# One wait a block for TensorE's weight halves, in place of one for the bank and one for each half

## The chip, the cores and the metric

The kernel runs on one core of a Trainium2 chip. The metric is the device time of one execution in microseconds; lower is better. The runs' times are of unprofiled executions; the profile is of one execution more.

## What is computed

One layer of a hybrid decoder for 256 prompt tokens and 8 sample tokens, 264 rows of 2048 features in all, in float32:

```
x = x + 1/2 * SwiGLU_1(rmsnorm(x))                    # 2048 -> 2 x 5632 -> 2048
h = rmsnorm(x);  P = h @ w_in                         # RWKV-7 columns | attention q,k,v | branch gates
A = RWKV-7 time mixing;  B = dilated window attention
x = x + (sigmoid(gA) * (A @ w_branch_rwkv) + sigmoid(gB) * (B @ w_branch_attn)) @ w_out
x = x + 1/2 * SwiGLU_2(rmsnorm(x))
```

Nearly all of TensorE's time goes into the products with the weights. To keep float32 precision with the float32r format of TensorE, each weight and each activation is split into a high part (rounded to float32r) and a low part (the rest), and each product of two 128-row tiles is three matmuls: high x high, high x low and low x high.

## The kernel before, in words

**Blocks, halves, quarters.** The weights are cut into 397 blocks, one for each 128 output features of a phase. A block has KT tiles of 128 x 128 (16 in most phases, 12 in the last part of each FFN's second matrix, 8 in `ba`, 6 in `bb`). It accumulates in one of four PSUM banks (`result`, block number modulo 4). The phases are, in order: `ffn1_in0`, `ffn1_out0`, `ffn1_in1`, `ffn1_out1`, `ffn1_in2`, `ffn1_out2`, `lora`, `qkv`, `rkv`, `gates`, `bb`, `ba`, `out`, and the six of the second FFN. A block is loaded in two halves. Half h of block b is unit u = 2b + h. A half of 16-tile blocks is 8 tiles, so 24 matmuls of 264 columns. `products` can also do a block's quarters apart, so that other work of TensorE stands between them; `rkv` and `gates` use this.

**The stream of a unit.** There are four slots (`RING`) for a unit's raw weights, high part and low part: `raw`, `whi`, `wlo`. SyncE's queue loads unit u into `raw` once the low part of unit u-4 has been made (`lo_done`). ScalarE's `split_hi` copies it to `whi`, once it has landed and TensorE is done with unit u-4 (`half_done`). VectorE's `split_lo` subtracts to make `wlo` and raises `lo_done`. TensorE multiplies and raises `half_done` at the end of each half.

**Order on ScalarE and VectorE.** The order is written out by hand. At step n of a phase each of the two first calls `ahead`, which splits the two units 2b + 3 and 2b + 4 (b is the block of step n, `LOOK` is 3), and then does what block n leaves: VectorE evicts the bank and raises `evac`. So the low part of unit 2b + 1 is made in the step of block b - 1, after the eviction of block b - 2 in most phases and of block b - 4 in all. In the first phase of each FFN the normalisation comes in between: TensorE sums the squares (`sums_pe`, line 335) after block 2, ScalarE takes the root and VectorE the reciprocal, and only then VectorE evicts blocks 0, 1 and 2 (`hidden` with n == 2), with ScalarE's `gate_silu` for blocks 0 and 2 in the same step. In step 0 of the first FFN ScalarE squares the second half of x and VectorE adds up the squares (`x_squares_dve`, lines 309 to 313).

**In the middle of the layer.** `qkv` has four groups of four small matmuls of TensorE (line 1268) that wait for ScalarE's sigmoids of the last group. In `rkv` TensorE does attention between the halves of some blocks: scores (line 1444), transposes (line 1456), values. When `bb` is done, GpSimd's queue loads the residual x back from memory (line 645), which VectorE needs in `out`.

**Loops.** `walk` runs most blocks of a phase in a hardware loop of four blocks a turn, so the thresholds of the waits hold a register there. Blocks outside the loops wait for constants.

Of the kernel before, what the change touches and what calls it, by code (L numbers as in the profile page):

```python
# [63 lines left out]
BODY = 4  # L64
# [98 lines left out]
def build(nc, ins, outs, side, xs):  # L163
    with ExitStack() as ctx:
# [11 lines left out]
        def sem(name):  # L176
            return ctx.enter_context(nc.semaphore(name))
# [29 lines left out]
        lo_done = sem("lo_done")  # L207
        half_done = sem("half_done")
        evac = sem("evac")
# [7 lines left out]
        act, dve, pe = nc.scalar, nc.vector, nc.tensor  # L217
# [23 lines left out]
        def products(name, n, i, parts, before=None, quarters=(0, 1, 2, 3)):  # L241

            b = FIRST[name] + n
            tiles = [(bank, k, kt, xhi, xlo) for bank, kt, xhi, xlo in parts for k in range(kt)]
            assert len(tiles) == KT_OF[b]
            h = len(tiles) // 2
            if 0 in quarters:
                pe.wait_ge(evac, b + 1 + BODY * i)
            for q in quarters:
                u = 2 * b + q // 2  # L250
                if q % 2 == 0:
                    pe.wait_ge(lo_done, u + 1 + 2 * BODY * i)
                for c in range(h // 2, h) if q % 2 else range(h // 2):
                    bank, k, kt, xhi, xlo = tiles[q // 2 * h + c]
                    if before is not None:
                        before(q // 2 * h + c)
                    hi, lo = (t[:, u % RING, c * P:(c + 1) * P] for t in (whi, wlo))
                    pe.matmul(bank[:, 0:T], hi, xhi[:, k], start=(k == 0), stop=False)  # L258
                    pe.matmul(bank[:, 0:T], hi, xlo[:, k], start=False, stop=False)  # L259
                    mm = pe.matmul(bank[:, 0:T], lo, xhi[:, k], start=False, stop=(k == kt - 1))  # L260
                if q % 2:
                    mm.then_inc(half_done, 1)
# [83 lines left out]
        def ffn_pe(f, r):  # L346
            for q, kt in enumerate(FFN_PARTS):
                first = q == 0
                pairs = (FT if f == 2 else 0) + sum(FFN_PARTS[:q])

                def hidden_there(k):
                    if k == 0 or k >= kt - 2:
                        pe.wait_ge(mid_done, pairs + max(k + 1, kt - 2))

                def up_down(n, i):
                    products(f"ffn{f}_in{q}", n, i, [(result(f"ffn{f}_in{q}", n), DT, hhi, hlo)],
                             h_there(r) if n == 0 and first else None)
                    if n == 2 and first:
                        sums_pe(r)
                walk(pe, f"ffn{f}_in{q}", up_down, BODY if first else 0)  # L360
                walk(pe, f"ffn{f}_out{q}", lambda n, i: products(
                    f"ffn{f}_out{q}", n, i, [(result(f"ffn{f}_out{q}", n), kt, mhi, mlo)],
                    hidden_there if n == 0 else None))
# [853 lines left out]
        def stream(name, hi, lo, before=None):  # L1217
            walk(pe, name, lambda n, i: products(name, n, i, [(result(name, n), KT_OF[FIRST[name]], hi, lo)],
                                                 before if n == 0 else None))
# [525 lines left out]
```

## Time and profile before

| | |
|---|---|
| median of 3 runs | 2451.45 us (2451.36 to 2454.17) |
| profiled execution | 2462.51 us, span 2460.7 us |
| TensorE busy | 2408.8 us, 98% of the span |
| VectorE busy | 1476.6 us, 60% |
| ScalarE busy | 974.7 us, 40% |
| mean granted TensorE clock | 0.985 |
| DMA | 428.27 MB, 174 GB/s |
| the chain that ended last | TensorE 92%, VectorE 3%, ScalarE 2%, DMA 2% |

Times in the trace are microseconds from the start of the span. A row of the timeline begins with an instruction's start and its duration; matmuls overlap in the pipeline, so a matmul of 0.28 us is followed by the next after 0.12 us. In brackets stands how long the engine was idle before, and what ended that.

### The profile page before, as it was taken

How to read it: one execution, taken by the hardware profiler on the slowest of the kernel's cores; microseconds unless marked ns; L12 is line 12 of the kernel's file. 1: busy time of each engine (PE TensorE's matmuls, PEld its weight loads, DVE VectorE, ACT ScalarE, POOL GpSimd, SP SyncE). 2: the span in 40 equal slices, each digit the busy share in tenths (PEclk: the TensorE clock that was granted, in tenths of full speed). 3: DMA queues.
4: the chain of work that ended last, by engine and by line, in shares of the span. 5: the costliest groups of instructions: out<-in, count | busy, mean ns of one | idle time of the engine just before them, and what ended most of it. 6: DMA issues, size and time to landing. Idle time of an engine off the chain costs nothing.

```text
span 2460.7 us, 57958 instructions
## 1 busy us (share of the span) xinstructions
PE 2408.8 (98%) x23350; PEld 2376.8 (97%) x23350; DVE 1476.6 (60%) x2071; ACT 974.7 (40%) x1233; POOL 81.4 (3%) x134
## 2 busy tenths in 40 slices
PE   7999999999999999979999999999999999999999
PEld 7999999999999999968999989999999999999999
DVE  6555555545567496666555585766555455555554
ACT  5333334333345543344222244644433333333333
POOL 0000000000013000000000000021000000000000
PEclk9999999999999999889999999999999999999999
DMA  6666566555556644323422454665555555555555
GB/s 236 207 226 201 183 226 228 182 182 183 179 162 231 210 156 138 106 97 126 144 80 80 147 174 133 217 193 169 192 186 180 180 182 181 183 180 180 183 167 172
DMA packets 122612, 428.27 MB, mean 174 GB/s; under 512 B 14296, under 2 KB 20568, under 8 KB 121440
## 3 DMA queue, kind: packets, MB, share of 16 engines
q1 hardware_dynamic: 117504, 393.49, 48.7%
q0 software_dynamic: 4960, 32.61, 3.9%
q8 instruction: 117, 1.92, 0.3%
q14 instruction: 31, 0.25, 0.0%
HBM read 415.17 MB, written 21.33 MB: 177 GB/s over the span
## 4 chain that ended last, share of the span: by engine, by line
PE 92%; DVE 3%; ACT 2%; DMA 2%; DVEq 1%; issue 1%; SPq 0%; ACTq 0%
PE bank L258 28%; PE bank L259 28%; PE bank L260 28%; PE bank L1225 4%; DVE wlo L231 1%; DMA raw<-in_weights 1%; ACT whi L225 1%; PE bank L1382 0%; PE bank L1420 0%; DMA x<-in_x 0%; PE bank L1549 0%; PE bank L1568 0%; PE bank L1561 0%; DVE nrm L1052 0%; DVE pr L1062 0%
## 5 line engine op out<-in xcount | busy, mean ns | idle before, releaser
L231 DVE TENSOR_TENSOR wlo<-raw,whi 128x1024 fp32r<-128x1024 f32 (+3 forms) x794 | 914.7, 1155 | 666.0 <-ACT whi L225 663.0
L258 PE MATMUL bank<-hhi,whi 128*128 128x264 f32 x4048 | 1171.1, 289 | 12.6 <-DVE hlo L294 12.6
L259 PE MATMUL bank<-hlo,whi 128*128 128x264 f32 x4048 | 1154.2, 285 | 0.0
L225 ACT ACTIVATE whi<-raw 128x1024 fp32r<-128x1024 f32 (+3 forms) x794 | 793.1, 1001 | 908.4 <-PE bank L260 880.2
L260 PE MATMUL bank<-hhi,wlo 128*128 128x264 f32 x4048 | 1152.8, 285 | 0.0
L258 PEld LDWEIGHTS bank<-hhi,whi 128*128 128x128 f32 x4048 | 769.9, 190 | 24.6 <-DMA ones<-in_ones 12.6
L259 PEld LDWEIGHTS bank<-hlo,whi 128*128 128x128 f32 x4048 | 770.5, 190 | 0.9
L260 PEld LDWEIGHTS bank<-hhi,wlo 128*128 128x128 f32 x4048 | 766.3, 189 | 0.0
L258 PE MATMUL bank<-mhi,whi 128*128 128x264 f32 x1408 | 399.5, 284 | 0.0
L260 PE MATMUL bank<-mhi,wlo 128*128 128x264 f32 x1408 | 399.0, 283 | 0.0
L259 PE MATMUL bank<-mlo,whi 128*128 128x264 f32 x1408 | 398.9, 283 | 0.0
L259 PEld LDWEIGHTS bank<-mlo,whi 128*128 128x128 f32 x1408 | 265.3, 188 | 0.0
L258 PEld LDWEIGHTS bank<-mhi,whi 128*128 128x128 f32 x1408 | 265.2, 188 | 0.0
L260 PEld LDWEIGHTS bank<-mhi,wlo 128*128 128x128 f32 x1408 | 264.0, 188 | 0.0
L372 ACT ACTIVATE silu<-gated 128x264 f32<-128x264 f32 x88 | 37.3, 424 | 203.7 <-DVE gated L417 203.7
L433 DVE SCALAR_TENSOR_TENSOR x<-bank,x 128x264 f32 (+1 forms) x96 | 41.5, 433 | 58.8 <-PE bank L260 58.8
L258 PE MATMUL bank<-mghi,whi 128*128 128x264 f32 x256 | 72.6, 284 | 0.0
L259 PE MATMUL bank<-mglo,whi 128*128 128x264 f32 x256 | 72.5, 283 | 0.0
L260 PE MATMUL bank<-mghi,wlo 128*128 128x264 f32 x256 | 72.5, 283 | 0.0
L417 DVE TENSOR_TENSOR gated<-bank,rstd 128x264 f32<-128x264 f32 x88 | 38.1, 433 | 48.0 <-PE bank L260 47.9
L288 ACT ACTIVATE hhi<-x,gains 128x264 fp32r<-128x264 f32 (+1 forms) x48 | 23.4, 512 | 77.0 <-DVE x L1019 40.3
L294 DVE SCALAR_TENSOR_TENSOR hlo<-x,gains,hhi 128x264 fp32r<-128x264 f32 (+1 forms) x48 | 32.4, 695 | 33.0 <-ACT hhi L288 32.9
(279 smaller groups left out, 1789.2 us busy)
## 6 DMA issues: line engine op xcount, KB each, us to landing
raw<-in_weights SPq DMA_DIRECT2D x666, 512.0 KB, 3.3
raw<-in_weights SPq DMA_DIRECT2D x64, 384.0 KB, 3.1
out_skv<-in_cache POOLq DMA_DIRECT2D x16, 512.0 KB, 3.9
raw<-in_weights SPq DMA_DIRECT2D x32, 256.0 KB, 2.8
raw<-in_weights SPq DMA_DIRECT2D x32, 192.0 KB, 2.5
side<-stg POOLq DMA_DIRECT2D x18, 132.0 KB, 3.6
gates<-side POOLq DMA_DIRECT2D x1, 2376.0 KB, 14.7
x<-in_x SPq DMA_DIRECT2D x4, 528.0 KB, 7.2
```

Of the source, the lines that this page charges most:

```text
L225: act.activation(whi[:, u % RING, 0:n], raw[:, u % RING, 0:n], ACT.Copy).then_inc(hi_done, 1)
L231: dve.tensor_tensor(wlo[:, s, 0:n], raw[:, s, 0:n], whi[:, s, 0:n].bitcast(F32), ALU.subtract).then_inc(lo_done, 1)
L258: pe.matmul(bank[:, 0:T], hi, xhi[:, k], start=(k == 0), stop=False)
L259: pe.matmul(bank[:, 0:T], hi, xlo[:, k], start=False, stop=False)
L260: mm = pe.matmul(bank[:, 0:T], lo, xhi[:, k], start=False, stop=(k == kt - 1))
L288: act.activation(hhi[:, m], x[:, m], ACT.Copy, scale=gained(r, n, i)).then_inc(hhi_done, 1)
L294: dve.scalar_tensor_tensor(hlo[:, m], x[:, m], gained(r, n, i), hhi[:, m].bitcast(F32), ALU.mult, ALU.subtract).then_inc(h_done, 1)
L372: act.activation(silu[:, n // 2 % 2], gated[:, n // 2 % 2], ACT.Silu).then_inc(silu_done, 1)
L417: dve.tensor_tensor(gated[:, slot], result(name, n)[:, 0:T], rstd[:], ALU.mult).then_inc(evac, 1)
L433: dve.scalar_tensor_tensor(x[:, m], result(out, n)[:, 0:T], 0.5, x[:, m], ALU.mult, ALU.add).then_inc(evac, 1)
L1225: mm = pe.matmul(out, lhs(j, p ^ frm), rhs(j, p ^ frm), start=(t == 0), stop=(t == len(terms) - 1))
```

## The change

Before, TensorE waits at the start of a block until the bank is free (`evac`), then for the low part of the block's first half, and in the middle for the low part of its second half. The low parts are made in order, so that the count that tells of the second half's tells of the first half's too, and VectorE's order puts the eviction of the bank's last block before it. After the change TensorE waits once, at the start of the block, until the low part of the second half is there. Block 0 is left as it was for its halves: it waits for its first half at its start and for its second in the middle.

```diff
@@ -244,12 +244,14 @@
             h = len(tiles) // 2
+
+
             if 0 in quarters:
-                pe.wait_ge(evac, b + 1 + BODY * i)
+                pe.wait_ge(lo_done, 2 * b + (2 if b else 1) + 2 * BODY * i)
             for q in quarters:
                 u = 2 * b + q // 2
-                if q % 2 == 0:
-                    pe.wait_ge(lo_done, u + 1 + 2 * BODY * i)
+                if q == 2 and b == 0:
+                    pe.wait_ge(lo_done, 2)
                 for c in range(h // 2, h) if q % 2 else range(h // 2):
```

## Rows read from the trace of the kernel before

**Rows 1.** The page: the span, and TensorE's line of busy times.

```profile
span 2460.7 us, 57958 instructions
...
PE 2408.8 (98%) x23350; PEld 2376.8 (97%) x23350; DVE 1476.6 (60%) x2071; ACT 974.7 (40%) x1233; POOL 81.4 (3%) x134
```

**Rows 2.** TensorE's sequencer at the lines of the waits: count, then ns min/median/max.

```profile
L252 PEldq ALU_OP  x441: 32/32/42, 38.7 to 2436.2; - x147
L252 PEldq EVENT_SEMAPHORE  x143: 51/51/51, 10.0 to 2451.4; - x143
...
L248 PEldq ALU_OP  x189: 32/32/32, 41.9 to 2434.0; - x189
```

**Rows 3.** Timeline of TensorE: the last matmuls of three halves in a row.

```profile
310.76 0.28 PE L260 MATMUL bank<-hhi,wlo 128*128 128x264 f32 x1
...
313.66 0.28 PE L260 MATMUL bank<-hhi,wlo 128*128 128x264 f32 x1
...
316.56 0.28 PE L260 MATMUL bank<-hhi,wlo 128*128 128x264 f32 x1
```

**Rows 4.** Timeline, second FFN part: a second half's split, and its block's first matmul.

```profile
301.35 1.23 DVE L231 TENSOR_TENSOR wlo<-raw,whi 128x1024 fp32r<-128x1024 f32 x1 [1.44 <-ACT whi L225]
...
305.08 0.28 PE L258 MATMUL bank<-hhi,whi 128*128 128x264 f32 x1
```

**Rows 5.** Timeline, first stage: block 2's first matmul, its second half's split.

```profile
25.95 0.28 PE L258 MATMUL bank<-hhi,whi 128*128 128x264 f32 x1
...
26.67 1.22 DVE L231 TENSOR_TENSOR wlo<-raw,whi 128x1024 fp32r<-128x1024 f32 x1
```

**Rows 6.** Timeline, first stage, block 4: first matmul, split, its middle's two matmuls.

```profile
38.00 0.28 PE L258 MATMUL bank<-hhi,whi 128*128 128x264 f32 x1
...
39.76 1.23 DVE L231 TENSOR_TENSOR wlo<-raw,whi 128x1024 fp32r<-128x1024 f32 x1 [1.44 <-ACT whi L225]
...
41.04 0.39 PE L258 MATMUL bank<-hhi,whi 128*128 128x264 f32 x1
41.26 0.28 PE L259 MATMUL bank<-hlo,whi 128*128 128x264 f32 x1
```

**Rows 7.** Timeline, second FFN, block 4: first matmul, second half's split.

```profile
1715.32 0.28 PE L258 MATMUL bank<-hhi,whi 128*128 128x264 f32 x1
...
1716.65 1.23 DVE L231 TENSOR_TENSOR wlo<-raw,whi 128x1024 fp32r<-128x1024 f32 x1 [1.44 <-ACT whi L225]
```

**Rows 8.** Timeline, bb, blocks 2 and 14: second half's split, first matmul.

```profile
1513.33 0.55 DVE L231 TENSOR_TENSOR wlo<-raw,whi 128x384 fp32r<-128x384 f32 x1
...
1513.54 0.28 PE L258 MATMUL bank<-obh,whi 128*128 128x264 f32 x1
...
1539.76 0.56 DVE L231 TENSOR_TENSOR wlo<-raw,whi 128x384 fp32r<-128x384 f32 x1
...
1540.02 0.28 PE L258 MATMUL bank<-obh,whi 128*128 128x264 f32 x1
```

**Rows 9.** Timeline of TensorE, ba, block 2: first matmul, first of the second half.

```profile
1550.25 0.29 PE L258 MATMUL bank<-oah,whi 128*128 128x264 f32 x1
...
1556.81 0.59 PE L258 MATMUL bank<-oah,whi 128*128 128x264 f32 x1 [4.94 <-DVE wlo L231]
```

**Rows 10.** Timeline, out, block 0: second half's split, first matmul.

```profile
1598.32 1.22 DVE L231 TENSOR_TENSOR wlo<-raw,whi 128x1024 fp32r<-128x1024 f32 x1
...
1598.84 0.28 PE L258 MATMUL bank<-mghi,whi 128*128 128x264 f32 x1
```

**Rows 11.** Timeline of TensorE: stalls in qkv and in rkv.

```profile
819.68 1.82 PE L1268 MATMUL bank<-lora,w2a 64*128 64x264 f32 x8 [2.08 <-ACT wlog L676]
...
1059.17 1.22 PE L1444 MATMUL bank<-qkv 64*128 64x128 f32 x4 [9.13 <-ACT pt L849]
```

**Rows 12.** Stretches: us, engines' busy us and counts, granted clock, DMA, GB/s.

```profile
821.70:825.20 3.50, 3.50 (x18) 3.50 (x18) 2.71 (x3) 2.41 (x5) 0.00 (x0) 0.51 0.74 209
...
1555.60:1562.40 6.80, 5.59 (x25) 5.59 (x26) 5.37 (x11) 4.09 (x9) 0.00 (x0) 0.50 0.49 156
```

## The prediction

> **What bounds the kernel now.** I read the page first. The span is 2460.7 us and TensorE is busy in 98% of it [rows 1]; the reader is to see that no other engine can be the bound of the whole, so that any time in which TensorE now stands still, or stops standing still, goes into the result almost one for one. The profiled execution took 2462.51 us with what lies around its span, the median of the runs is 2451.45 us; I work out a difference in the profiled execution and add it to the median.
>
> Then the sequencer side of the waits: what the removed instructions cost. In the looped blocks the thresholds are computed in registers, and the trace shows these as operations of TensorE's sequencer: 189 at the line of the bank's wait, 441 at the line of the half's wait, of 32 ns each, and 143 stand-alone waits of 51 ns [rows 2]. Then the pace of the matmuls. The last matmul of a half starts at 310.76, that of the next half at 313.66, of the one after at 316.56: 2.90 us for 24 matmuls both times, 120.8 ns for one [rows 3]. The first of the two halves is the second of its block, which waits once; the other begins a block, and a turn of the loop as well, and waits twice. They take the same time. So the sequencer runs ahead of the matmuls and what it does for a wait that is already met costs nothing.
>
> Then how early the low parts are ready. A wait costs only if the split is late, so I set the end of each of VectorE's 794 operations that write the low part beside the first matmul of the block that it belongs to. The pattern of most blocks is [rows 4]: the low part of the second half of the block that starts at 305.08 ended at 301.35 + 1.23 = 302.58, 2.50 us before the block began. Waiting for it at the start of the block is free there. But in 15 of the 397 blocks the second half's low part ends after the block has started. The kernel of before hides that behind the first half's matmuls. The changed one doesn't.
>
> **The change, part by part.**
>
> The bank's wait goes. VectorE evicts the bank's last block before it makes the low part now waited for, so the new wait implies it, and TensorE never idled for an eviction before one of these blocks. Its sequencer work is worth nothing by [rows 3]. The least it can be worth is nothing; the most, if each register operation and wait delayed the matmuls by its whole duration, is 189 x 32 ns, half of 441 x 32 ns and 143 x 51 ns [rows 2], 20.4 us. I take nothing, since the two equal halves are the same case and the bound is not.
>
> The first half's wait is implied by the second's. The second half's wait moves to the start of the block. What queues behind it are the first half's 24 matmuls (9 to 18 where the blocks are shallower), and for these halves ScalarE's next split of the slot waits, then VectorE's, then SyncE's next load. Nothing moves on SyncE's or GpSimd's queue. Block 0 keeps its two waits.
>
> So the price is a sum over the late blocks. For each: the end of the low part, less the start of the block, plus the 0.05 us in which TensorE takes the news (40.99 to 41.04 in [rows 6]), less the stall in the middle that goes away.
>
> First stage, blocks 1 and 2. Block 2 starts at 25.95; its second low part runs from 26.67 to 27.89, behind VectorE's sums of squares of x [rows 5]: 1.99 us. Those sums hang on x's load and not on TensorE, so the smaller lateness of block 1 is inside this.
>
> First stage, block 4. Starts at 38.00; low part 39.76 to 40.99; the middle stall of before was 41.04 less 38.00 less 2.90, 0.14 us [rows 6]. Price 3.04 - 0.14 = 2.90 us. Why it is late decides whether this adds to the last one: ScalarE's and VectorE's order puts the root, the reciprocal and the first gate blocks ahead of this split, and all of them wait for the sum that TensorE makes after block 2. The chain moves with block 2, so it adds. Block 5 is late by 1 us as well, but its low part doesn't wait for block 4's matmuls, and the 2.90 us cover it.
>
> Second FFN, block 4: the same chain. Start 1715.32, low part 1716.65 to 1717.88 [rows 7]: 2.61 us. Block 5 is covered again.
>
> bb, blocks 2 and 14: 1513.54 against 1513.88, and 1540.02 against 1540.32 [rows 8]: 0.39 and 0.35 us.
>
> ba, block 2. Here GpSimd's queue issues x's reload, the whole residual, once bb is done, and the weights land behind it. TensorE starts the block at 1550.25, does its first half of 12 matmuls, and stands until 1556.81, 4.94 us of it idle [rows 9]. Now it stands from the start of the block until the same 1556.81, and the 12 matmuls, 12 x 0.1208 = 1.45 us, come after. ba's block 0 is late too (0.9 us), but this stall takes that up.
>
> out, block 0: 1598.84 against 1598.32 + 1.22 = 1599.54 [rows 10]: 0.75 us.
>
> lora's block 2 (0.1 us) and qkv's block 2 (0.7 us) stand before a stall of 2.08 us in which TensorE waits for ScalarE, itself held by weights that land late; rkv's blocks 12 and 13 (1.5 us, since TensorE's transposes stand between the halves there) before one of 9.13 us on ScalarE's and VectorE's attention chain [rows 11]. These I cost at nothing: the cover is those stalls, and without it they would be 2.3 us.
>
> A restart: after a stall the second matmul comes 0.22 us behind the first (41.04 to 41.26) in place of 0.12 [rows 6]. Five of the stalls are new (first block 2, second FFN, the two of bb, out): 5 x 0.10 = 0.50 us.
>
> Sum: 1.99 + 2.90 + 2.61 + 0.39 + 0.35 + 1.45 + 0.75 + 0.50 = 10.94 us. 2451.45 + 10.94 = 2462.4 us, and about 2473.5 us for a profiled execution.
>
> **The clock, weighed against a rule.** After this stall of 4.94 us in ba the granted clock is 0.50 (1.2 GHz) for 6.80 us, with 25 matmuls in it [rows 12]; at full clock these take 25 x 0.12 = 3.0 us of the 5.59 us that they took, so the drop costs about 2.6 us. After the stall in qkv and the few small matmuls behind it the clock was 0.51 over 3.50 us [rows 12], with 18 matmuls where 3.50 / 0.12 = 29 would fit: 11 x 0.12 = 1.3 us. The stalls that my forecast adds to the FFN are 3.0 and 2.6 us long, between these two, with dense matmuls on either side. The Trainium skill (TensorE: Matmul & The Clock Gate, HAM oscillation) has waits between bursts of matmuls put the engine back to the lower clock, burst after burst; it speaks against this change. By it each of the two long stalls would also cost a drop; the trace has that after its longest stalls, and none with an isolated stall of 3 us, so it doesn't decide.
>
> **The rivals.**
> A, my forecast: the stalls as summed, no new drop of the clock. 2462.4 us.
> B, the clock falls as well. For it: the two rows of [rows 12]. Against: the new stalls are shorter than ba's, and isolated. 1.3 to 2.6 us for each of the two: 2463.7 to 2467.6 us, with one of them at the mean price 2464.3.
> C, the lateness that hangs on transfers is a thing of the profiled execution, which took 11 us longer than the median. Then the first block 2, bb's block 14, ba and out lose little, and what the order of the engines' own work makes late stays: 2.90 + 2.61 + 0.39 and two restarts, 6.1 us: 2457.6 us. Against: the weights pass the same queues without the profiler.
> D, the other side: faster. TensorE's sequencer is late somewhere, and the matmuls pay for its instructions. From 11 us of such instructions on it outweighs the stalls; at its 20.4 us the time is 2451.45 - 20.4 + 10.9 = 2442.0 us. Against: the two equal halves [rows 3].
> E, the change loses next to nothing: VectorE's chain ahead of block 4 turns out not to move with block 2, or shifts are taken up in later stalls as in [rows 11]. Half of the sum gone, under 4.9 us: about 2455 us.
>
> **How the numbers follow.** A 0.51, B 0.27, C 0.10, D 0.04, E 0.08. The likeliest is A. The range reaches from C's time to B's upper one, 2457.5 to 2467.6, and leaves out D, E and a part of B and C. A measurement of this kernel can tell about 0.2%, 4.9 us, from no change: A, B and C are slower by more, E is within, D is faster. Slower 0.88, same 0.08, faster 0.04.
>
> **What the changed kernel's profile would show.** Right: TensorE's first matmul of block 2 about 0.05 us after the end of the low part, near 27.9, and no idle in the middle of a block past block 0; a stall of 3 us ahead of block 4 in both FFNs; in ba the stall of before moved from the middle of block 2 to its start, with 24 matmuls after it; fewer sequencer operations at the two lines and the same 2.90 us from half to half. Wrong: halves shorter than 2.90 us (D); block 4 starting on time (E); new stretches at 1.2 GHz behind the FFN stalls (B). What would make the number wrong while the mechanism holds is that transfers land at other times, and that a stretch of low clock begins or ends elsewhere than before.

## The result

The changed kernel takes 2468.22 us (median of 6 runs, 2466.71 to 2474.78), the kernel before 2452.55 us (median of 6, 2449.93 to 2462.33): slower, ratio 1.0063, interval 1.0043 to 1.0083, or 10.5 to 20.4 us. The forecast was 2462.4 us, 2457.5 to 2467.6. The sign, the mechanism and the larger stalls were right; the median lies 0.6 us above the range, whose upper end was rival B's. The profiled execution took 2474.78 us, 12.3 us more than the profiled one of before.

The page of the changed kernel, to [rows 1]: 652 instructions fewer, and TensorE busy 5.8 us longer with the same 23350 matmuls.

```profile
span 2473.0 us, 57306 instructions
...
PE 2414.6 (98%) x23350; PEld 2381.1 (96%) x23350; DVE 1477.7 (60%) x2071; ACT 975.8 (39%) x1233; POOL 81.4 (3%) x134
```

The sequencer's operations at the line of the one wait, to [rows 2]. The 441 operations and 143 stand-alone waits at the halves' line are gone.

```profile
L250 PEldq ALU_OP  x189: 32/32/42, 46.3 to 2446.3; - x189
```

Three halves in a row, to [rows 3]. 2.90 us for each, as before, though most of the sequencer's work for the waits is gone: it had cost nothing.

```profile
315.17 0.28 PE L262 MATMUL bank<-hhi,wlo 128*128 128x264 f32 x1
...
318.07 0.28 PE L262 MATMUL bank<-hhi,wlo 128*128 128x264 f32 x1
...
320.97 0.28 PE L262 MATMUL bank<-hhi,wlo 128*128 128x264 f32 x1
```

What TensorE waited for, over the whole execution: us in total, times, the longest.

```profile
PE bank L1446 <- ACT pt L851: 20.0, 3, 7.8
PE bank L260 <- DVE wlo L231: 12.7, 7, 3.7
...
PE bank L1332 <- issue: 0.5, 1, 0.5
PE bank L1227 <- issue: 0.2, 1, 0.2
```

Waits for a low part are now seven, 12.7 us; the kernel before had one, of 4.94 us ([rows 9]). Here are the matmuls behind six of the seven, and the splits that the first two waited for, to [rows 5] to [rows 10].

```profile
26.09 1.22 DVE L231 TENSOR_TENSOR wlo<-raw,whi 128x1024 fp32r<-128x1024 f32 x1
...
27.36 0.39 PE L260 MATMUL bank<-hhi,whi 128*128 128x264 f32 x1 [1.07 <-DVE wlo L231]
...
41.26 1.23 DVE L231 TENSOR_TENSOR wlo<-raw,whi 128x1024 fp32r<-128x1024 f32 x1 [1.44 <-ACT whi L225]
...
42.54 0.39 PE L260 MATMUL bank<-hhi,whi 128*128 128x264 f32 x1 [2.87 <-DVE wlo L231]
...
1521.65 0.40 PE L260 MATMUL bank<-obh,whi 128*128 128x264 f32 x1 [0.24 <-DVE wlo L231]
...
1565.31 0.59 PE L260 MATMUL bank<-oah,whi 128*128 128x264 f32 x1 [3.74 <-DVE wlo L231]
...
1606.76 0.39 PE L260 MATMUL bank<-mghi,whi 128*128 128x264 f32 x1 [0.97 <-DVE wlo L231]
...
1725.93 0.39 PE L260 MATMUL bank<-hhi,whi 128*128 128x264 f32 x1 [2.45 <-DVE wlo L231]
```

Each is the first matmul of a block, and starts 0.05 us after the split ends (41.26 + 1.23 = 42.49, then 42.54). They are block 2 and block 4 of the first FFN, block 2 of bb, block 3 of ba (the forecast had block 2), block 0 of out, block 4 of the second FFN. The seventh is rkv's block 12, and what follows it is to [rows 11]:

```profile
1045.96 0.39 PE L260 MATMUL bank<-hhi,whi 128*128 128x264 f32 x1 [1.37 <-DVE wlo L231]
...
1063.73 0.58 PE L1446 MATMUL bank<-qkv 64*128 64x128 f32 x1 [7.81 <-ACT pt L851]
```

The stall of 9.13 us in block 13 is now 7.81 us: it took up the 1.37 us, as forecast.

The clock, in four stretches of the changed kernel, to [rows 12]: two in gates, one after the other, one in ba behind the stall, and one behind the second FFN's stall.

```profile
1227.00:1232.30 5.30, 5.30 (x102) 5.08 (x99) 1.97 (x4) 1.54 (x2) 0.54 (x1) 1.00 0.44 153
1232.40:1235.80 3.40, 3.40 (x58) 3.16 (x58) 0.00 (x0) 1.06 (x1) 0.00 (x0) 0.51 0.21 83
1564.10:1570.30 6.20, 4.99 (x22) 4.99 (x23) 4.23 (x8) 3.62 (x8) 0.00 (x0) 0.50 0.45 135
1727.30:1730.70 3.40, 3.40 (x18) 3.40 (x18) 2.35 (x5) 0.27 (x1) 0.00 (x0) 0.51 0.81 265
```

The low clock of the second and of the last is new against the kernel before. In the last there are 18 matmuls in 3.40 us at 1.2 GHz, where 28 fit at full clock. The one in gates stands behind no stall: the first line shows TensorE busy in all of the 5.30 us ahead of it.

A stretch from one block's first matmul to a later one's can be compared over all traces, whatever its place in time. Here are the us of each.

| stretch | before, twice | changed, twice | the change |
|---|---|---|---|
| first FFN, block 1 to 3 | 11.85, 11.85 | 13.19, 13.57 | 1.34, 1.72 |
| first FFN, block 3 to 8 | 29.44, 29.46 | 32.34, 33.90 | 2.90, 4.46 |
| qkv, block 2 to 4 | 18.53, 19.96 | 18.51, 15.29 | none, scatters |
| rkv, block 0 to its end | 240.2, 240.2 | 240.1, 239.6 | none |
| gates, block 0 to its end | 346.3, 346.3 | 349.4, 347.3 | 3.2, 1.1 |
| bb, to block 15 | 33.10, 33.10 | 33.62, 33.62 | 0.52 |
| ba, block 0 to 4 | 19.37, 18.14 | 17.94, 17.13 | scatters |
| ba block 4 to out block 1 | 40.86, 42.50 | 42.05, 41.94 | 1.1 over the lower |
| second FFN, block 0 to 8 | 46.86, 46.86 | 51.12, 49.58 | 4.26, 2.72 |
| the rest of the FFNs | equal to 0.01 | equal to 0.01 | nothing |

The second values are from the repetitions below. Gates' 3.2 us are pauses of 1.6 us in all, at three places where nothing released TensorE, and 1.6 us for the stretch at 1.2 GHz; its 1.1 us are pauses alone. Both profiled executions of the kernel before lay some 10 us over its median, with long stretches in qkv and ba, where transfers set the stalls.

### The profile page after: what moved, and what is told of

Same layout as the page of the kernel before. It is cut to its first block, busy times and chain, and to the rows that moved or that the text cites. A ratio compares the mean times of both kernels' runs of the same rounds, so it can differ in the third digit from the quotient of the medians.

```text
span 2473.0 us, 57306 instructions
## 1 busy us (share of the span) xinstructions
PE 2414.6 (98%) x23350; PEld 2381.1 (96%) x23350; DVE 1477.7 (60%) x2071; ACT 975.8 (39%) x1233; POOL 81.4 (3%) x134
## 4 chain that ended last, share of the span: by engine, by line
PE 90%; DVE 4%; ACT 2%; DMA 2%; issue 1%; DVEq 1%; SPq 0%; ACTq 0%
PE bank L260 28%; PE bank L261 27%; PE bank L262 27%; PE bank L1227 4%; DVE wlo L231 2%; DMA raw<-in_weights 1%; ACT whi L225 1%; PE bank L1384 0%; PE bank L1422 0%; PE bank L1551 0%; PE bank L1570 0%; DMA x<-in_x 0%; PE bank L1563 0%; DVE nrm L1054 0%; DVE pr L1064 0%
## 6 DMA issues: line engine op xcount, KB each, us to landing
gates<-side POOLq DMA_DIRECT2D x1, 2376.0 KB, 14.2
```

## The experiments

The question was which blocks the difference stands in, and what is in it beyond the stalls as summed. Theory 1: the stalls ahead of late blocks are all of it. Theory 2: waiting once costs something also where nothing is late. Unless a diff says otherwise, each kernel is the one before, in which the phases of a list take the single wait:

```diff
+            once = name in ('ffn1_in0', 'ffn2_in0')
             if 0 in quarters:
-                pe.wait_ge(evac, b + 1 + BODY * i)
+                if once:
+                    pe.wait_ge(lo_done, 2 * b + (2 if b else 1) + 2 * BODY * i)
+                else:
+                    pe.wait_ge(evac, b + 1 + BODY * i)
             for q in quarters:
                 u = 2 * b + q // 2
-                if q % 2 == 0:
+                if not once and q % 2 == 0:
                     pe.wait_ge(lo_done, u + 1 + 2 * BODY * i)
+                elif q == 2 and b == 0:
+                    pe.wait_ge(lo_done, 2)
```

Each result below is a median, then the ratio to the kernel before on the same chip, with its interval in brackets, then that ratio as us. The us are good to some 2 to 4 either way; the plain difference of the medians is up to 2 us off them (10.6 in place of 8.6 for the second experiment, 4.5 in place of 3.4 for the fourth). So it is the traces that tell terms of 1 or 2 us apart.

**The changed kernel again.** No edit.

> The changed kernel once more, unaltered, to see which of its differences come back. Theory 1 (the stalls ahead of the late blocks make the whole difference): 11 to 14 us slower, the stalls of 1.3 and 3.1 us before blocks 2 and 4 of the first FFN and of 2.7 us before block 4 of the second come back; the 3.2 us that the first profile of it lost in gates, where no block waits for a low part, do not all come back, since they are a stretch of low clock (1.7 us) and three pauses of 0.3 to 0.7 us at single small matmuls. Theory 2 (the one wait also costs something where nothing is late): the 3.2 us in gates come back at the same places, and the time is 15 us or more over the kernel before.

2468.75 us, ratio 1.0059 (1.0043 to 1.0075), 14.5 us. The stalls came back, with 2.90 us ahead of block 4 in the first FFN and 2.72 in the second; so did part of the loss in gates: 1.1 us, at the same three matmuls, without the low clock there. The stretch of low clock was behind the first FFN's block 4 this time.

**The first phase of each FFN alone.** `once` as in the diff above.

> The single wait in the first phase of each FFN (ffn1_in0 and ffn2_in0) alone, the three waits everywhere else. Theory 1: 1.99 + 2.90 + 2.61 us and two restarts, 7.7 us slower by the forecast's own terms; 9.3 us if the clock falls behind the stall of the second FFN as in the first profile of the changed kernel. Theory 2: the same here, and what is missing to the whole change stands in the other phases.

2464.71 us, 1.0035 (1.0022 to 1.0048), 8.6 us. In the trace 2.90 us ahead of block 4 in the first FFN and 4.07 us in the second (50.93 less 46.86 for blocks 0 to 8), with low clock behind it. Its gates, which keep the three waits, take 1.5 us more than those of before: there is a stretch at 1.2 GHz in them, and no pause.

**lora, qkv, rkv and gates alone.** `once = name in ('lora', 'qkv', 'rkv', 'gates')`.

> The single wait in lora, qkv, rkv and gates alone. Theory 1: nothing, within 1.5 us, since the late blocks of qkv and rkv stand before longer stalls that take them up, and gates has none. Theory 2: 3 to 5 us slower, most of it in gates.

2457.31 us, 1.0013 (1.0003 to 1.0023), 3.2 us, between the two. The trace shows 0.2 us in lora and a pause of 0.3 us in gates and no more; the three kernels below that split this set give less.

**bb, ba and out alone.** `once = name in ('bb', 'ba', 'out')`.

> The single wait in bb, ba and out alone. By the forecast's terms 0.39 + 0.35 + 1.45 + 0.75 us and three restarts, 3.2 us slower. By the trace of the changed kernel, where the stall of ba came one block later and was 1.2 us shorter, about 0.3 us: bb 0.5, ba -1.4, out 1.1. Theory 2 has nothing to say of these blocks beyond the forecast's 3.2 us.

2458.62 us, 1.0014 (1.0005 to 1.0022), 3.4 us: the forecast's 3.2 us, and not the 0.3 us that one trace had suggested. Between ba's blocks 0 and 4 the seven traces with a single wait there take 17.1 to 20.2 us, 18.3 in the mean, and the eleven without 14.4 to 19.4, 16.7 in the mean. One pair of traces can't give this term: the difference of the means is 1.6 us, give or take 1.2.

**All waits, and the new one.** The kernel before, with one line more:

```diff
                 pe.wait_ge(evac, b + 1 + BODY * i)
+                pe.wait_ge(lo_done, 2 * b + (2 if b else 1) + 2 * BODY * i)
```

> All three waits of the kernel before, and the one of the changed kernel added to them at the start of each block: TensorE stands where the changed kernel stands, and its sequencer has more to do than in either. If what the removed waits cost is nothing, as the forecast had it (the equal halves), this takes the same time as the changed kernel, within 1.5 us. If the matmuls paid for the sequencer's register operations and waits, it is slower than the changed kernel by up to 20 us and more.

2469.23 us, 1.0054 (1.0041 to 1.0067), against 1.0059 and 1.0063 of the changed kernel. Four waits cost what one costs, within the 3 to 4 us of these intervals. The traces say it more sharply: the FFN phases beyond block 8 take 719.43 us in the first FFN and 715.07 in the second in all eighteen traces, with one, three or four waits a block. Only right behind a stall do the waits show: block 4 begins 3.24 us after the matmul before it, and 3.15 in the changed kernel. Its gates have none of the pauses, but a stretch at 1.2 GHz for 1.5 us.

**The FFNs' other phases alone.** `once` for the ten FFN phases other than `ffn1_in0` and `ffn2_in0`.

> The single wait in the ten FFN phases other than the first of each (ffn1_out0 to ffn1_out2, ffn2_out0 to ffn2_out2), where every second half's low part is ready 0.75 us or more before its block; 240 of the 397 blocks. Theory 1: the same as before, within 1 us, and halves of 2.90 us. If a wait removed is worth anything, it is faster; if waiting at the start of a block costs by itself, slower.

2456.53 us, 1.0010 (1.0000 to 1.0020). Those phases take the same to 0.01 us in the trace. What it has more is 2.6 us in gates, where its waits are those of before: a pause of 1.0 us and a stretch at 1.2 GHz. That is the 2.5 us of its ratio. With the three sets before it this one makes up all the blocks; together they give 17.7 us, against 14.5 and 15.5 us for the whole change. The intervals allow this, and what happens in gates doesn't add up set by set.

**The kernel before again.** No edit.

> The kernel before once more, unaltered, on the same chip: what the comparison shows for no change. Within 0.2% in its median; its profile shows how much single phases differ between two executions of one program. In gates, a stretch of low clock or pauses of some tenths of a microsecond at single small matmuls would show that these are not the change's.

2456.45 us, 1.0000 (0.9990 to 1.0009). In gates it agrees with the first trace to 0.1 us; between qkv's blocks 2 and 4 it takes 1.4 us more.

**lora and qkv alone.** `once = name in ('lora', 'qkv')`.

> The single wait in lora and qkv alone (21 blocks). The forecast: nothing, since qkv's block 2 is late only when its weights land late, and then ScalarE's sigmoids behind the same transfer hold TensorE in front of block 3 anyway; 0.2 us for lora's block 2, which every trace of a kernel with the single wait there shows. The rival: the delay is not taken up, 0.8 to 3 us slower.

2454.36 us, 0.9995 (0.9986 to 1.0004). lora's 0.2 us are in the trace; qkv's block 2 costs nothing.

**rkv alone.** `once = name == 'rkv'`.

> The single wait in rkv alone (24 blocks). The forecast: nothing, the wait of 1.6 us ahead of block 12 is taken up by the stall of 8 to 9 us in block 13. The rival: 1.5 us slower.

2454.48 us, 0.9997 (0.9987 to 1.0006). Taken up: the wait ahead of block 12 is there, and its first matmul comes 1.68 us after the one before. Block 12 is late in ten of the eighteen traces, by about 1.5 us in eight of them. In these eight, blocks 11 to 14 take 34.0 to 34.2 us in the five with the single wait, and in the three without it as well. In the two where it is late by 3 us they take 35.72 us with it and 35.73 without.

**gates alone.** `once = name == 'gates'`.

> The single wait in gates alone (32 blocks, none of them late). The forecast: nothing. The rival: pauses of TensorE of 0.1 to 0.7 us, at places where no wait stands and which come back from execution to execution, since the shorter program is cut otherwise as it is fetched: 0.3 to 1.1 us slower, with pauses at other matmuls than in the changed kernel.

2456.82 us, 1.0009 (0.9998 to 1.0020). Inconclusive in time; its trace has no pause, so the rival as I put it fell: a shorter gates doesn't have to pause.

**The first phases but for the loop's first place.** `once = name in ('ffn1_in0', 'ffn2_in0') and n != 4`.

> The single wait in ffn1_in0 and ffn2_in0, but for the blocks at the loop's first place (4, 8, 12, ...), which keep the three waits. The first FFN's stall ahead of block 2 stays, 1.4 us; the 3 us ahead of block 4 go; and block 5, whose lateness block 4's stall covered, now shows it: 0.96 + 0.05 us in the first FFN, 0.78 + 0.05 in the second, and 0.1 us each for the restart. 1.4 + 1.1 + 0.9 = 3.4 us slower than before, without a stretch of low clock in either FFN. If block 4's stall is not what makes the 8.6 us of the kernel with the single wait in all these blocks, it stays at 6 us or more.

2458.41 us, 1.0014 (1.0004 to 1.0023), 3.4 us. The first matmuls of block 5 in the two FFNs:

```profile
46.32 0.39 PE L264 MATMUL bank<-hhi,whi 128*128 128x264 f32 x1 [0.84 <-DVE wlo L231]
...
1713.84 0.39 PE L264 MATMUL bank<-hhi,whi 128*128 128x264 f32 x1 [0.67 <-DVE wlo L231]
```

With block 4's stall gone, block 5 stands. Blocks 3 to 8 take 30.58 us, 1.12 over those of before; the second FFN's 0 to 8 take 47.80, 0.94 over. No low clock in either. A late block that another covers costs nothing until the cover goes.

**The same stall, filled.** The single wait in the two first phases, and:

```diff
+                    if n == 3 and first:
+                        for k in range(16):
+                            pe.matmul(banks[4][:, 0:T], hhi[:, k, 0:P], hhi[:, k], start=True, stop=True)
```

> The single wait in ffn1_in0 and ffn2_in0, and 16 matmuls more behind block 3 of each, whose results nobody reads, into a bank that is free: TensorE works for 1.9 us of the 3 us for which it would stand ahead of block 4. The stall in time stays, what goes is the clock's reason to fall. If a stretch at 1.2 GHz behind one of the two stalls is what the single wait there costs beyond 7.2 us, as in each of the four traces so far with these stalls: no such stretch in this profile, and 1.5 us less than the 8.6 us measured without the added matmuls. If the stretches come for another reason, one is there again.

**The changed kernel, filled.** The same addition to the changed kernel.

> The changed kernel with the same 16 matmuls more behind block 3 of each FFN's first phase, results unread. No stretch at 1.2 GHz behind the stalls ahead of block 4 in either FFN, and 1.5 us less than the changed kernel's 14.5 us over the kernel before. If there is one again, the added matmuls don't keep the clock up and its price of 1.5 us is not tied to the length of the stall.

**The unfilled one beside them.** The second experiment's kernel again.

> The single wait in ffn1_in0 and ffn2_in0 alone, once more and on the chip of the two filled kernels, to stand beside them. 8.6 us slower than before as the first time, and a stretch at 1.2 GHz behind one of the two stalls ahead of block 4.

On one chip: filled 1.0035 (1.0022 to 1.0047), unfilled 1.0052 (1.0040 to 1.0064), the changed kernel filled 1.0055 (1.0042 to 1.0068). The filled kernel is 3 to 4 us under the unfilled one beside it, but the unfilled one's first measurement was 1.0035 as well: the 1.5 us that I expected against it are not there, and the unfilled one came out at 12.8 us in place of 8.6. The changed kernel, filled, is at 13.5 us, where 13.0 was expected. So the times alone don't decide. The traces do. Behind the first FFN's stall, unfilled and then filled:

```profile
44.00:47.30 3.30, 3.30 (x17) 3.30 (x17) 2.30 (x5) 0.08 (x1) 0.51 (x1) 0.50 0.92 319
```

```profile
42.90:46.30 3.40, 3.40 (x28) 3.40 (x29) 3.15 (x6) 0.77 (x2) 0.28 (x1) 1.00 0.60 187
```

17 matmuls against 28. In each of the seven traces with unfilled 3 us stalls, exactly one of the two had low clock behind it (five times the first FFN's, twice the second's; the two kernels below are among the seven); in the two traces with filled stalls none of four. Which of the two it is changes between executions of the same kernel. Both filled kernels had a stretch at 1.2 GHz in gates instead, worth about 1.5 us and behind no stall. Such a stretch in gates is in seven of the eighteen traces: in the first of the changed kernel and not in its second, in its filled form and the one with 96 waits, in the kernel with four waits, in three kernels whose gates have the three waits of before, and in neither trace of the kernel before. No experiment was made for its cause.

**The program moved.** 48 waits that are met at once, ahead of everything else on TensorE, and 96 in the second kernel:

```diff
+            for k in range(48):
+                pe.wait_ge(ones_in, 16)
             ffn_pe(1, 0)
```

> The changed kernel with 48 waits more at TensorE's start that are met at once, while the engine still has nothing to multiply: all that follows in its program moves by 48 instructions, and no wait or stall moves. Theory (the pauses of gates are the program's fetch): the pauses of 0.1 to 0.7 us at the three places where both traces of the changed kernel have them are gone, or stand at other matmuls or are of another length. Rival (they come from the waits or from the data): the same pauses at the same matmuls.

> The same with 96 waits. Theory: the places or lengths of the pauses in gates differ from those of the changed kernel and from those with 48. Rival: the same places and lengths in all. The time is that of the changed kernel within 2 us either way.

1.0055 (1.0036 to 1.0073) and 1.0077 (1.0059 to 1.0095). The pause stands in TensorE's list of waits as idle time that nothing released. The changed kernel, the one with 48, the one with 96:

```profile
PE bank L1332 <- issue: 0.5, 1, 0.5
```

```profile
PE bank L260 <- issue: 1.3, 1, 1.3
```

```profile
PE bank L260 <- issue: 2.3, 1, 2.3
```

The last of the three pauses stood behind the 14844th matmul of the program in both traces of the changed kernel (0.66 and 0.40 us), behind the 14832nd with 48 waits (1.45 us), behind the 14820th with 96 (2.36 us); the first went from the 9489th to the 9477th and was gone. No wait and no stall of gates was touched. So they hang on the program's length ahead of them.

The traces say more. The 48 waits stand in them as 24 instructions, and 12 matmuls with their weight loads are 24 as well. Counted in all of TensorE's instructions, the changed kernel pauses at 19206, 27398 and 29959 in both traces; with 48 waits, and with the 16 matmuls of its filled form, it pauses at 19206 and 29958, each time at another matmul of the program. Between these places lie 8192 and about 2560 instructions, 32 and 10 times 256. And every one of the 14 pauses in gates, over all traces, ends 2.2 to 2.6 us after a packet of 16384 bytes began on the queue that the page lists as "instruction"; in gates such a packet comes every 7 us or so. That these pauses are waits for the program's next piece is therefore well supported. What makes a piece late in one kernel and not in another was not tried.

The 96 waits missed my expectation for the time, within 2 us of the changed kernel: 18.9 us over the kernel before in place of 14.5. Neither the 48 nor the 96 were hidden, as I had thought: they run from about 12 us on, and TensorE's first matmul starts at 15.25 and 17.15 us in place of 12.05 and 12.47. The stall ahead of block 2 gives part of it back (blocks 1 to 3 take 12.15 and 11.92 us), so that block 3 starts at 35.39 and 37.65 us in place of 33.51 and 33.94. With the 96, that is about 4 us; the longer pause is 1.7 to 2.0 more.

## Why the prediction was off

**The mechanism held.** The time went where the sum put it: seven waits for a low part, each at the start of a block, each ending 0.05 us after the split. The removed waits were worth nothing (719.43 and 715.07 us for the FFNs' other blocks in every trace; 2.90 us for every half).

**The sum, term by term**, forecast and measured in us:

| term | forecast | measured |
|---|---|---|
| first FFN, block 2, with restart | 2.09 | 1.34, 1.72 |
| first FFN, block 4 | 2.90 | 2.90 |
| second FFN, block 4, with restart | 2.71 | 2.72 |
| bb, with restarts | 0.94 | 0.52 |
| ba | 1.45 | 1.6, give or take 1.2 |
| out, with restart | 0.85 | 1.1 |
| lora | 0 | 0.2 |
| qkv, rkv | 0 | 0 |
| clock behind an FFN stall | 0 | 1.5 |
| pauses in gates | 0 | 1.6, 1.1 |
| low clock in gates | 0 | 1.6, 0 |
| sum, with the mean where there are two | 10.94 | 14.2 |

The whole was 14.5 us by the second measurement, whose interval (10.6 to 18.4) holds the 14.2; single terms are not resolved by the times.

**What failed first: A was put above B.** The step was "it doesn't decide": the trace of before had no isolated stall of 3 us, and I let the forecast go without a drop and gave the drop 0.27. Every trace with these stalls unfilled has one, at 1.5 us (33.90 less 32.34, 51.12 less 49.58; 2.8 us in the trace with 48 waits, where the stretch was twice as long), inside the 1.3 to 2.6 us that B had from [rows 12], and never both. The rule of the Trainium skill that I weighed against it (TensorE: Matmul & The Clock Gate, HAM oscillation) speaks of a relapse burst after burst; here it came behind one stall of two, and 16 matmuls in the stall kept it away in four of four. A choice between rivals for something that falls by chance should have been a term at its expected size.

**What failed second: nothing was kept for the program's length.** A change that removes instructions moves all behind them. In this program that costs 0 to 2.5 us in gates, where the pauses stand at fixed counts of instructions, some 8192 and 2560 apart; no row of before could show it. With the low clock in gates these are 2.1 us in the mean of the two traces that the sum put at nothing, more than the drop behind the FFN's stall. B with one drop, 2464.3 us, is 3.9 us short of the measured median; these terms are 2.1 of them.

**Smaller.** Block 2 of the first FFN waits for a chain that begins with x's load, and block 1 starts when its own does; in the eight traces in which these blocks keep their three waits the lateness is 0.76 to 2.17 us, 1.94 in the one that I read, and where they take the single wait it costs 1.2 to 1.7 us (less with the 48 and 96 waits, which start TensorE later). bb's block 14 was late by 0.30 us in the first trace of the kernel before, by 0.07 in the second, and in no other. ba's late block is block 2 in the first trace of before and in one more; in the second trace of before it is block 3, as in all the others in which ba has a late block, whichever wait it has. So that was the execution and not the change, and the cost came out near the forecast's on the average. The covers held: rkv's and lora's and qkv's were tried alone, and block 5's by taking the cover away; only lora's 0.2 us came through.

**The other rivals.** C: that lateness hanging on transfers is a thing of the profile. Wrong in kind, but right in that the two profiles of before were some 10 us over their median, in qkv and ba above all; bb, ba and out alone cost 3.4 us unprofiled. D fell on the four waits and on the equal phases. E fell on the traces: block 4's chain moves with block 2. (E's number didn't follow from its words either: half of the sum is 5.5 us, not under 4.9.)

## What to carry to other kernels

A wait that is met costs nothing while the sequencer runs ahead of the matmuls, so there is nothing to win by removing it; one that comes earlier costs wherever its condition is late, and it is the few late blocks, not the usual slack of 2.5 us, that set the price. List the lateness of every block, cross out those whose cover is a later stall, and ask of each whether the one before it covers it. Add what a standing TensorE does to its clock as an expected cost, and take a stretch that hangs on transfers from several traces, not one.

## What was not expected of the hardware

A stall of TensorE of 3 us between dense matmuls drops the granted clock to 1.2 GHz for 3.4 us (6.8 us once) behind seven of fourteen such stalls, at about 1.5 us of time (2.8 us the long one); with 16 matmuls in it it did not in four of four. And 24 or 48 more instructions at the start of TensorE's program (48 or 96 waits in the source) moved pauses of up to 2.4 us, 14800 matmuls later, by 12 matmuls each time, and changed their length; without the shift they were 0.1 to 0.7 us long, and in the kernel before absent. They stay at the same count of TensorE's instructions, and end some 2.4 us after a packet of 16384 bytes began on the instruction queue.
